# The end of a two-layer mixture-of-experts kernel: last rows completed from rows stored early, gathers issued together

## The chip, the cores and the metric

The kernel runs on one core of one Trainium2 chip. The metric is the device time of the whole program in microseconds (us); of several runs the median is given. Lower is better. All data is float32.

## The reference, cut to what matters

The program is a two-layer backbone: attention, then a grouped top-2 mixture of experts (MoE), with residual additions, and a final RMSNorm. The part around the change is the MoE of the second layer, with the residual addition and the final norm:

```python
def rms_norm(x, g):
    return x * rsqrt(mean(x * x, axis=-1) + 1e-6) * g

# h: 1024 tokens x 1024; every token has two experts with a gate each
y = ragged_dot(silu(ragged_dot(h[tok], w_gate)) * ragged_dot(h[tok], w_up), w_down)
y = y * gate                       # one row per (token, expert)
moe = zeros_like(h).at[tok].add(y) # two rows per token are summed
xl = xl + mod_l[5] * moe
out = rms_norm(xl, final_norm)
```

## The kernel before, in words

Tokens are sorted to experts by slots: each (token, expert) has a slot, and the tensor `slot_out` (`ys`) in HBM holds one finished row per slot, already gated and scaled by the modulation row. The experts stage of a layer (`experts`, L1679 on) works through items. An item is one expert with up to some hundred slots, or a block of 64 or 128 further slots. In the second layer (l = 1) F = 14 items are written out, then a loop `Fori(F, n)` handles blocks of 64 rows (once in this run), and a last item, one block of 128 slots at LASTB, is written out by itself.

TensorE (`last_item`, L1919) computes eight blocks b of gate and up products (L1929; 16 products of 128 x 128 each), then two halves of the down product (L1937), then a small product (L1942) that moves the rows of the last item to the place of the same tokens in a tile of their own. ACT takes silu of each block (L2050), VectorE multiplies it with the up part (`product`, L2163). Block b + 2 on TensorE waits for product b, since both use the same PSUM banks; the down products wait for the eighth product. Weights come in six pieces of 2 MB per item (`load_piece`, L1434 on: four of gate and up in two transfers each, two of down in one each), issued by SP into a ring of six buffers as soon as a piece's buffer is free.

While the last item is computed, the other tokens are finished. There are LT = 8 tiles t of 128 tokens. GpSimd gathers a tile's two rows per token from `slot_out` (`pairs`, L1808, indirect DMAs of 512 KB at L1813) into `pair[t]`: for the first tiles spare buffers, for tiles 3 to 7 ring buffers that must be free (`freed`, waits on `s_gu`). VectorE adds the two rows and then adds them to the residual x (`combined`, L2165, additions L2167 and L2169). ACT squares and sums (`square`, L2052). GpSimd takes the root (`root`, L1816, lines L1817 and L1819), VectorE scales (`scaled`, L2171, line L2176), and SP stores the tile (L1775). The slots of the last item are held at zero in `slot_out` (stored at L1754), so that all of this can run before the last item has a result.

The up to 128 tokens of the last item need their result added. Before: ACT stores each summed tile x to `x_rows` in HBM after its square (L2055, 8 stores of 512 KB). When all are stored, GpSimd gathers the 128 tokens' rows from `x_rows` into `zrow` (L1833). VectorE adds the small product (L2207, two halves), ACT squares (L2064), GpSimd takes the root, VectorE scales (L2211), and GpSimd scatters the rows to the output (L1839) when the eight tiles' stores have landed.

The order of work is written out by hand: each engine has one program, and semaphores tie them. GpSimd: pairs 0 to 2, then for each t: pairs t + 3, wait for the square of t, root t; then the gather from `x_rows`. ACT: silu 0 to 3, then for each t: square t, store t, silu t + 4. VectorE: products 0 to 2, combined 0, product 3, combined 1, then for b = 4 to 7: product b, combined b - 2, scaled b - 4; then the rest of combined and scaled with the two halves of gated rows (`gated_rows`, L2179, line L2183) between.

Of the kernel before, what the change touches and what calls it, by code (L numbers as in the profile page):

```python
# [8 lines left out]
I32 = mybir.dt.int32  # L9
# [4 lines left out]
P = 128  # L14
# [121 lines left out]
def build(nc, a):  # L136
# [3 lines left out]
    toep = dram("toep", [3, BLOCK_W, 16 * DROWS, BLOCK_W])  # L140
    h_dram = dram("h_rows", [NTOK, D])
    x_rows = dram("x_rows", [SEQ, D])
    ys = dram("slot_out", [-(-max(SLOTS) // P) * P, D])

    top = ExitStack()
# [21 lines left out]
    with top:  # L167
# [1511 lines left out]
        def experts(l, ring, p_in, token, gate, xg, s_xg):  # L1679
# [31 lines left out]
            with ExitStack() as c:  # L1711
# [12 lines left out]
                if l == 1:  # L1724
                    at_z = rows[:, 2, HALF:HALF + 4]
                    at_zi = slots[:, LT:NT, :].rearrange("p t i -> p (t i)")
                    flat = lambda q, r: ring[:, q, :, :].rearrange("p k f -> p (k f)")[:, r * D:(r + 1) * D]
                    pair = ((x[:, LT, :], x[:, LT + 1, :]), (yr[:, 1, :], yr[:, 2, :]), (xg[:, 1, :], xg[:, 2, :]),
                            (flat(0, 0), flat(0, 1)), (flat(0, 2), flat(0, 3)), (flat(1, 0), flat(1, 1)), (flat(1, 2), flat(1, 3)),
                            (flat(2, 0), flat(2, 1)))  # L1730
                    freed = (0, 0, 0, 2, 2, 4, 4, 6)
                    zrow, zjunk = flat(2, 2), flat(2, 3)
                    same = aT[:, 0, P:2 * P]
                    final_row = rows[:, 1, :]
                    s_pair = [sem(c, f"y_in{n}") for n in range(LT)]
                    (s_zero, s_zs, s_nr, s_xz, s_zx, s_zxT, s_zc, s_id, s_sum, s_x, s_ss, s_rs, s_h, s_xs, s_out, s_back, s_my, s_zz,
                     s_zss, s_zo, s_fin) = (sem(c, n) for n in (
                        "last_zero", "last_cleared", "final_row_in", "last_x_gathered", "last_x_transposed", "last_xT_ready", "last_token_steps",
                        "last_tokens_along", "pair_sum", "x_added", "ss_done", "rstd_steps", "out_rows", "x_stored", "out_stored",
                        "last_x_back", "last_shared", "last_x_steps", "last_ss", "last_out", "last_out_stored"))  # L1740
                block = c.enter_context(nc.Block())
                gub = lambda j, b, w: bank((b % 2) * 2 + w, 0, room(j))
                yb = lambda j, d: bank(4 + d % 2, 0, room(j))
# [4 lines left out]
                @block.sync  # L1748
                def _(sp):
                    n = count(sp)  # L1750
                    if l == 1:
                        sp.dma_start(final_row, a["final_norm"].partition_broadcast(P)).then_inc(s_nr, 16)
                        sp.wait_ge(s_zero, 1)
                        sp.dma_start(ys[SLOT0[l][F]:SLOT0[l][F] + P, :], yr[:, 2, :]).then_inc(s_zs, 16)  # L1754

                    with sp.Fori(1, n) as i:
                        e = sp.value_load(table[0:1, bass.ds(i, 1)], min_val=0, max_val=NE - 1)
                        for q in range(6):

                            if q < 4:  # L1760
                                sp.wait_ge(s_gu, i * 8 + 2 * q + 2)
                            else:
                                sp.wait_ge(s_y, i * 8 + 4 * (q - 4) + 4)
                            load_piece(sp, l, ring, p_in, e, q)
                    if l == 1:
                        e = sp.value_load(table[0:1, 63:64], min_val=0, max_val=NE - 1)
                        for q in range(6):
                            if q < 4:
                                sp.wait_ge(s_gu, n * 8 + 2 * q + 2)
                            else:  # L1770
                                sp.wait_ge(s_y, n * 8 + 4 * (q - 4) + 4)
                            load_piece(sp, l, ring, p_in, e, q)
                        for t in range(LT):
                            sp.wait_ge(s_h, t + 1)
                            sp.dma_start(grid_rows(out[0], t), pair[t][0]).then_inc(s_out, 16)  # L1775
                        sp.wait_ge(s_out, 16 * LT)
# [19 lines left out]
                def _(pool):  # L1796
                    n = count(pool)
                    pool.sem_inc(s_xt, 4)
                    for j in range(1, F + 1):
                        gather(pool, j)  # L1800
                        if l == 1 and j == F - 2:
                            nc.gpsimd.indirect_dma_start(out=xg[:, 1, :], out_offset=None, in_=h_dram,
                                                         in_offset=bass.IndirectOffsetOnAxis(token[:, LASTB:LASTB + 1], 0)).then_inc(s_xz, 16)
                    with pool.Fori(F, n) as j:
                        gather(pool, j + 1)
                    if l == 1:
# [15 lines left out]
                        pool.wait_ge(s_zx, 4)  # L1822
                        pool.wait_ge(s_st, OLD_ST + stored(n))
                        pool.sem_inc(s_go, 1)
                        for t in range(3):
                            pairs(t)
                        for t in range(LT):
                            if t + 3 < LT:
                                pairs(t + 3)
                            pool.wait_ge(s_ss, t + 1)  # L1830
                            root(t)
                        pool.wait_ge(s_xs, 16 * LT)
                        nc.gpsimd.indirect_dma_start(out=zrow, out_offset=None, in_=x_rows,  # L1833
                                                     in_offset=bass.IndirectOffsetOnAxis(token[:, LASTB:LASTB + 1], 0)).then_inc(s_back, 16)
                        pool.wait_ge(s_zss, 1)
                        root(LT)
                        pool.wait_ge(s_zo, 1)
# [175 lines left out]
                def _(act):  # L2013
# [32 lines left out]
                    if l == 1:  # L2046
# [5 lines left out]
                        def square(t):  # L2052
                            act.wait_ge(s_x, t + 1)
                            nc.scalar.activation(pair[t][1], x[:, t, :], ACT.Square, accum_out=ss[:, t:t + 1]).then_inc(s_ss, 1)
                            act.dma_start(x_rows[t * P:(t + 1) * P, :], x[:, t, :]).then_inc(s_xs, 16)  # L2055

                        for b in range(4):
                            silu(b)
                        for t in range(LT):
                            square(t)  # L2060
                            if t + 4 < FB:
                                silu(t + 4)
                        act.wait_ge(s_zz, 2)
                        nc.scalar.activation(zjunk, zrow, ACT.Square, accum_out=ss[:, LT:LT + 1]).then_inc(s_zss, 1)  # L2064
                    act.wait_ge(s_st, OLD_ST + stored(n))
# [3 lines left out]
                def _(dve):  # L2069
# [89 lines left out]
                    def last_item():  # L2159
# [23 lines left out]
                            nc.vector.scalar_tensor_tensor(out=yr[:, 0, cols], in0=bank(4 + h), scalar=gate[:, 0, LASTB:LASTB + 1],  # L2183
                                                           in1=rows[:, 0, cols], op0=ALU.mult, op1=ALU.mult).then_inc(s_yr, 1)

                        for b in range(3):
                            product(b)
                        combined(0)
                        product(3)
                        combined(1)  # L2190
                        for b in range(4, FB):
                            product(b)
                            combined(b - 2)
                            scaled(b - 4)
                        combined(6)
                        scaled(4)
                        combined(7)
                        gated_rows(0)
                        scaled(5)
                        scaled(6)  # L2200
                        gated_rows(1)
                        scaled(7)
                        dve.wait_ge(s_back, 16)
                        for h in range(2):
                            cols = slice(h * HALF, (h + 1) * HALF)
                            dve.wait_ge(s_my, h + 1)
# [116 lines left out]
```

## Time and profile before

| | |
|---|---|
| median of 3 runs | 4063.71 us (4054.61, 4063.71, 4065.64) |
| the profiled execution, its own time | 4054.0 us |
| its span | 4052.2 us |
| TensorE busy (matmul) | 3765.5 us, 93% |
| VectorE busy | 1239.8 us, 31% |
| ACT busy | 760.5 us, 19% |
| GpSimd busy | 404.1 us, 10% |
| read from and written to HBM | 547.56 MB and 77.47 MB |

The profile is one execution, recorded instruction by instruction; its span is from the first to the last instruction. Times in it are counted from the start of the span. Engines are PE (TensorE matmuls), PEld (TensorE weight loads), DVE (VectorE), ACT (ScalarE), POOL (GpSimd) and SP; a name with q, as SPq, is that engine's issue of a DMA. DMA queue q1 is SP's, q10 is ACT's, q0 is GpSimd's. An f32 matmul is recorded as two instructions, so a block of 16 products is 32 records. "issue" as the reason of a wait means that the profile shows nothing that the engine waited for. DMA figures are of packets that move over 16 transfer engines.

### The profile page before, as it was taken

To read this page: it belongs to the slowest core of one execution; us is meant where nothing else is said; L and a number is where in the kernel's file an instruction comes from. 1 tells how busy PE (TensorE), PEld (TensorE's weight loads), DVE (VectorE), ACT (ScalarE), POOL (GpSimd) and SP (SyncE) were. 2 spreads that over 40 slices of the span, in tenths; PEclk is the share of its full clock that TensorE was granted. 3 is DMA by queue.
4 is the path that set the end of the run, shared out by engine and by line. 5 is a ranking of instruction groups with operands and counts; after the bars stand their busy time and mean duration, and the time that the engine had idled before them with its cause. 6 is when DMAs were issued, how large, how long until landed. Compare 5 with 4: busy or idle time off the path is not lost. (4 is left out here: it accounts for less than half of the span.)

```text
span 4052.2 us, 53671 instructions
## 1 busy us (share of the span) xinstructions
PE 3765.5 (93%) x22338; PEld 2858.8 (71%) x22338; DVE 1239.8 (31%) x3166; ACT 760.5 (19%) x1668; POOL 404.1 (10%) x400
## 2 busy tenths in 40 slices
PE   6999999999699999999958999999989699999996
PEld 3656767645577899998835666666655678899774
DVE  3233333322411112211153555555532401101113
ACT  2222333311000000000022333333321000000001
POOL 3001000023000000000031111011014000000002
PEclk7999999998799999999969999999998799999998
DMA  5458500110744466779741000000101748867988
GB/s 161 164 210 327 188 21 26 53 35 39 250 141 146 164 204 231 263 264 306 261 145 33 12 16 17 17 16 16 48 12 42 258 160 271 289 206 254 316 296 323
DMA packets 450551, 628.09 MB, mean 155 GB/s; under 512 B 25928, under 2 KB 343752, under 8 KB 444048
## 3 DMA queue, kind: packets, MB, share of 16 engines
q1 hardware_dynamic: 420504, 514.83, 38.4%
q0 software_dynamic: 21008, 79.37, 5.3%
q10 hardware_dynamic: 8808, 30.49, 2.1%
q8 instruction: 183, 3.00, 0.3%
q14 instruction: 48, 0.39, 0.0%
HBM read 547.56 MB, written 77.47 MB: 154 GB/s over the span
## 5 line engine op out<-in xcount | busy, mean ns | idle before, releaser
L1960 PE MATMUL ps<-item_xT,expert_ring 128*128 128x128 f32 (+9 forms) x7168 | 1054.4, 310 | 1.1 <-DVE item_xT L2078 1.1
L1960 PEld LDWEIGHTS ps<-item_xT,expert_ring 128*128 128x128 f32 x7168 | 1000.3, 191 | 56.9 <-issue 5.5
L1997 PE MATMUL ps<-item_aT,expert_ring 128*128 128x144 f32 (+8 forms) x2304 | 405.1, 331 | 0.0
L1997 PEld LDWEIGHTS ps<-item_aT,expert_ring 128*128 128x128 f32 x2304 | 356.9, 192 | 24.1
L2223 DVE TENSOR_TENSOR item_aT<-item_silu,ps 128x128 f32<-128x128 f32 (+9 forms) x224 | 74.5, 333 | 962.1 <-ACT item_silu L2034 962.1
L2034 ACT ACTIVATE item_silu<-ps 128x128 f32<-128x128 f32 (+9 forms) x224 | 70.2, 313 | 1150.1 <-PE ps L1960 1150.1
L732 PE MATMUL ps<-hT,w_group 128*128 128x512 f32 (+1 forms) x704 | 254.7, 515 | 0.5 <-PEq L297 0.5
L377 PE MATMUL ps<-hT,oT 128*128 128x512 f32 x576 | 251.5, 596 | 1.4 <-PEq L982 0.7
L1076 PE MATMUL ps<-hT,w_group 128*128 128x512 f32 (+1 forms) x576 | 232.4, 546 | 0.5 <-PEq L297 0.5
L377 PEld LDWEIGHTS ps<-hT,oT 128*128 128x128 f32 x576 | 109.2, 191 | 134.7 <-issue 134.7
L1790 POOL DMA_INDIRECT gathered<-h_rows,slot_tokens x48 | 49.5, 1031 | 1542.9 <-PE ps L1868 1537.1
L1125 PE MATMUL ps<-df_kT,df_qT 64*128 64x512 f32 (+1 forms) x768 | 188.3, 567 | 14.9 <-DVE df_max L1354 8.5
L732 PEld LDWEIGHTS ps<-hT,w_group 128*128 128x128 f32 x704 | 130.4, 190 | 100.8 <-issue 95.0
L1076 PEld LDWEIGHTS ps<-hT,w_group 128*128 128x128 f32 x576 | 106.1, 190 | 99.8 <-issue 97.3
L1141 PEld LDWEIGHTS ps<-df_V,rows 128*128 128x128 f32 x1280 | 154.0, 195 | 17.9 <-issue 16.1
L1141 PE MATMUL ps<-df_V,rows 128*128 128x128 f32 x1280 | 157.5, 279 | 0.9 <-ACT rows L1268 0.9
L1085 PE MATMUL ps<-w_group,hT 128*128 128x128 f32 x1280 | 152.1, 277 | 0.0
L1085 PEld LDWEIGHTS ps<-w_group,hT 128*128 128x128 f32 x1280 | 146.3, 192 | 7.0 <-issue 7.0
L741 PE MATMUL ps<-w_group,hT 128*128 128x128 f32 x1280 | 146.5, 275 | 0.0
L741 PEld LDWEIGHTS ps<-w_group,hT 128*128 128x128 f32 x1280 | 144.7, 192 | 0.1
L1354 DVE CUSTOM_DVE_ANT_0 rows<-ps,df_zero 128x512 f32<-128x512 f32 x180 | 107.8, 599 | 120.3 <-PE ps L1125 120.3
L1987 PE MATMUL ps<-expert_ring,item_aT 128*128 128x512 f32 x320 | 139.1, 593 | 0.0
(315 smaller groups left out, 3951.4 us busy)
## 6 DMA issues: line engine op xcount, KB each, us to landing
expert_ring<-in_expert_w_gate SPq DMA_DIRECT2D x128, 1024.0 KB, 5.2
expert_ring<-in_expert_w_up SPq DMA_DIRECT2D x128, 1024.0 KB, 8.1
expert_ring<-in_expert_w_down SPq DMA_DIRECT2D x64, 2048.0 KB, 9.8
oT<-in_mod_w SPq DMA_DIRECT2D x40, 1024.0 KB, 6.4
slot_out<-rows POOLq DMA_DIRECT2D x9, 4096.0 KB, 39.2
w_group<-in_w_qkv SPq DMA_DIRECT2D x48, 512.0 KB, 3.8
slot_out<-item_y ACTq DMA_DIRECT2D x31, 512.0 KB, 7.5
h_rows<-hr SPq DMA_DIRECT2D x18, 512.0 KB, 2.6
```

Of the source, the lines that this page charges most:

```text
L377: m = nc.tensor.matmul(bank(n % 3), oT[:, k * NTOK + t * P:k * NTOK + (t + 1) * P], wo[:, k, h * HALF:(h + 1) * HALF], start=k == 0, stop= ...
L732: m = nc.tensor.matmul(bank(b, 0, w), wq[:, 0 if kind == "q" else 1, k, :], hT[:, k, c0:c0 + w], start=k == 0, stop=k == KD - 1)
L741: m = nc.tensor.matmul(bank(b, t * P, (t + 1) * P), hT[:, k, (c0 + t) * P:(c0 + t + 1) * P], wq[:, 2, k, :], start=k == 0, stop=k == KD - 1)
L1076: m = nc.tensor.matmul(bank(b, 0, w), wq[:, 0 if kind == "q" else 1, k, :], hT[:, k, c0:c0 + w], start=k == 0, stop=k == KD - 1)
L1085: m = nc.tensor.matmul(bank(b, t * P, (t + 1) * P), hT[:, k, (c0 + t) * P:(c0 + t + 1) * P], wq[:, 2, k, :], start=k == 0, stop=k == KD - 1)
L1125: nc.tensor.matmul(S(m, n), qT[r, par, t * P:(t + 1) * P], kT[r, par, c0:c0 + w], start=True, stop=True).then_inc(s_S, 1)
L1141: mm = nc.tensor.matmul(O, pT[:, i * P:(i + 1) * P], V[:, par, i, :], start=i == 0, stop=i == NT - 1)
L1354: nc.vector.tensor_tensor_reduce(out=maps(g, t)[m][:, c0:c0 + w], in0=S(m, n), in1=zero[:, 0:1].to_broadcast([P, w]), scale=1.0, scalar=NE ...
L1960: m = nc.tensor.matmul(gub(j, b, w), ring[:, b // 2, k, w * 256 + (b % 2) * P:w * 256 + (b % 2 + 1) * P], xT[:, k, 0:C], start=k == 0, sto ...
L1987: m = nc.tensor.matmul(bank(4 + h)[0:C], aT[:, f, 0:C], ring[:, 4 + h, f, :], start=f == 0, stop=f == FB - 1)
L1997: m = nc.tensor.matmul(yb(j, d), ring[:, 4 + d // 4, f, (d % 4) * P:(d % 4 + 1) * P], aT[:, f, 0:C], start=f == 0, stop=f == FB - 1)
L2223: nc.vector.tensor_tensor(aT[:, b, 0:C], sg[:, b % 2, 0:C], gub(j, b, 1), ALU.mult).then_inc(s_a, 1)
```

## The change

- A small tensor `slot_pairs` in HBM takes each token's two slots. SP stores it, and the eight tiles of x as they are before the experts' sum, into `x_rows`, at the start of the second layer's experts stage.
- GpSimd gathers the two slots of each of the last item's tokens into `at_zi[:, 0:2]`, ahead of its loop, and waits for them.
- GpSimd issues all eight pairs ahead of the first root. At t = 2 of its loop over roots, when all gate and up blocks are done, it gathers the last tokens' residual rows from `x_rows` and their two rows each from `slot_out`, into ring buffers 2 and 3.
- ACT no longer stores x. It takes silu 0 to 5, then for each t: silu t + 6, square t.
- VectorE takes products 0 to 5, combined 0, product 6, combined 1, product 7, and then the rest in the order of the diff. After the eighth scaling it adds the two gathered rows to `zrow`, one after the other, before the halves of L2207.

```diff
@@ build @@
+    slot_pairs = dram("slot_pairs", [SEQ, 2], I32)
@@ experts, l == 1 @@
+                    zpair = (flat(3, 0), flat(3, 1))
@@ sync @@
                         sp.wait_ge(s_zero, 1)
                         sp.dma_start(ys[SLOT0[l][F]:SLOT0[l][F] + P, :], yr[:, 2, :]).then_inc(s_zs, 16)
+                        sp.dma_start(slot_pairs.rearrange("(t p) i -> p t i", p=P), slots[:, 0:LT, :]).then_inc(s_xs, 16)
+                        for t in range(LT):
+                            sp.dma_start(x_rows[t * P:(t + 1) * P, :], x[:, t, :]).then_inc(s_xs, 16)
@@ gpsimd @@
+                    if l == 1:
+                        pool.wait_ge(s_xs, 16 * (LT + 1))
+                        pool.wait_ge(s_zc, 4)
+                        nc.gpsimd.indirect_dma_start(out=at_zi[:, 0:2], out_offset=None, in_=slot_pairs,
+                                                     in_offset=bass.IndirectOffsetOnAxis(token[:, LASTB:LASTB + 1], 0)).then_inc(s_pz, 16)
+                        pool.wait_ge(s_pz, 16)
                     with pool.Fori(F, n) as j:
                         gather(pool, j + 1)
...
-                        for t in range(3):
+                        for t in range(LT):
                             pairs(t)
                         for t in range(LT):
-                            if t + 3 < LT:
-                                pairs(t + 3)
+                            if t == 2:
+                                pool.wait_ge(s_gu, n * 8 + 16)
+                                pool.sem_inc(s_go, 1)
+                                nc.gpsimd.indirect_dma_start(out=zrow, out_offset=None, in_=x_rows,
+                                                             in_offset=bass.IndirectOffsetOnAxis(token[:, LASTB:LASTB + 1], 0)).then_inc(s_back, 16)
+                                for i in range(2):
+                                    nc.gpsimd.indirect_dma_start(out=zpair[i], out_offset=None, in_=ys,
+                                                                 in_offset=bass.IndirectOffsetOnAxis(at_zi[:, i:i + 1], 0)).then_inc(s_back, 16)
                             pool.wait_ge(s_ss, t + 1)
                             root(t)
-                        pool.wait_ge(s_xs, 16 * LT)
-                        nc.gpsimd.indirect_dma_start(out=zrow, out_offset=None, in_=x_rows,
-                                                     in_offset=bass.IndirectOffsetOnAxis(token[:, LASTB:LASTB + 1], 0)).then_inc(s_back, 16)
@@ scalar @@
-                            act.dma_start(x_rows[t * P:(t + 1) * P, :], x[:, t, :]).then_inc(s_xs, 16)
-
-                        for b in range(4):
+
+                        for b in range(6):
                             silu(b)
                         for t in range(LT):
+                            if t + 6 < FB:
+                                silu(t + 6)
                             square(t)
-                            if t + 4 < FB:
-                                silu(t + 4)
@@ vector @@
-                        for b in range(3):
+                        for b in range(6):
                             product(b)
                         combined(0)
-                        product(3)
+                        product(6)
                         combined(1)
-                        for b in range(4, FB):
-                            product(b)
-                            combined(b - 2)
-                            scaled(b - 4)
+                        product(7)
+                        for t in range(2, 5):
+                            combined(t)
+                            scaled(t - 2)
+                        gated_rows(0)
+                        combined(5)
+                        scaled(3)
                         combined(6)
-                        scaled(4)
+                        gated_rows(1)
                         combined(7)
-                        gated_rows(0)
-                        scaled(5)
-                        scaled(6)
-                        gated_rows(1)
-                        scaled(7)
-                        dve.wait_ge(s_back, 16)
+                        for t in range(4, LT):
+                            scaled(t)
+                        dve.wait_ge(s_back, 48)
+                        for i in range(2):
+                            if i:
+                                dve.wait_ge(s_zy, 1)
+                            nc.vector.tensor_tensor(zrow, zrow, zpair[i], ALU.add).then_inc(s_zy, 1)
+                        dve.wait_ge(s_zy, 2)
```

## Rows read from the trace of the kernel before

**Rows 1.** The page's head.

```profile
span 4052.2 us, 53671 instructions
```

**Rows 2.** The chain that ended last: start us, us, what.

```profile
4011.38 14.47 DMA expert_ring<-slot_out,slots
...
4031.99 7.77 DMA expert_ring<-x_rows,slot_tokens
...
4039.79 1.30 DVE expert_ring L2207 x2
...
4044.90 1.06 POOL out L1839
```

**Rows 3.** DMA queues: packets, MB; from 3987.5 to 3990, 4000 to 4002.5, 2060 to 2064.

```profile
q1 hardware_dynamic: 181, 0.34, 36.6%
q0 software_dynamic: 177, 0.66, 66.4%
...
q10 hardware_dynamic: 88, 0.29, 29.1%
...
q0 software_dynamic: 399, 1.46, 95.8%
```

**Rows 4.** Timeline of POOL: start us, us, what, [idle before and what ended it].

```profile
3931.52 0.18 POOL L1785 COPY item_tokens<-slot_tokens 128x1 int32 x1 [42.26 <-PE ps L1868]
...
3980.20 0.95 POOL L1813 DMA_INDIRECT x_res<-slot_out,slots  x1 [46.77 <-DMA slot_out<-item_y]
...
3996.61 1.54 POOL L1813 DMA_INDIRECT expert_ring<-slot_out,slots  x1 [0.18 <-issue]
...
4010.05 1.02 POOL L1813 DMA_INDIRECT expert_ring<-slot_out,slots  x1 [0.27 <-issue]
```

**Rows 5.** Timeline of DVE.

```profile
3990.92 1.23 DVE L2167 TENSOR_TENSOR x_res<-x_res 128x1024 f32<-128x1024 f32 x1 [7.87 <-DMA x_res<-slot_out,slots]
...
3993.32 0.28 DVE L2163 TENSOR_TENSOR item_aT<-item_silu,ps 128x128 f32<-128x128 f32 x1
...
4010.82 1.23 DVE L2167 TENSOR_TENSOR expert_ring<-expert_ring 128x1024 f32<-128x1024 f32 x1 [1.74 <-DMA expert_ring<-slot_out,slots]
4012.09 1.23 DVE L2169 TENSOR_TENSOR x_res<-x_res,expert_ring 128x1024 f32<-128x1024 f32 x1
4013.23 1.28 DVE L2176 SCALAR_TENSOR_TENSOR gathered<-x_res,rstd,rows 128x1024 f32<-128x1024 f32 x1
...
4028.28 0.74 DVE L2183 SCALAR_TENSOR_TENSOR item_y<-ps,rows 128x512 f32<-128x512 f32 x1
...
4028.94 2.47 DVE L2176 SCALAR_TENSOR_TENSOR expert_ring<-x_res,rstd,rows 128x1024 f32<-128x1024 f32 x2
```

**Rows 6.** Timeline of PE and of ACT.

```profile
3971.43 18.35 PE L1929 MATMUL ps<-item_xT,expert_ring 128*128 128x128 f32 x156
3990.91 0.50 PE L1929 MATMUL ps<-item_xT,expert_ring 128*128 128x128 f32 x3 [1.14 <-issue]
...
3993.65 13.93 PE L1929 MATMUL ps<-item_xT,expert_ring 128*128 128x128 f32 x96 [1.75 <-DVE item_aT L2163]
...
3982.45 0.28 ACT L2050 ACTIVATE item_silu<-ps 128x128 f32<-128x128 f32 x1 [3.30 <-PE ps L1929]
3990.96 0.28 ACT L2050 ACTIVATE item_silu<-ps 128x128 f32<-128x128 f32 x1 [8.23 <-DMA expert_ring<-in_expert_w_down]
```

**Rows 7.** Windows: us, engines busy (x instructions), granted PE clock, DMA share, GB/s.

```profile
3180.00:3200.00 20.00, 16.15 (x85) 14.03 (x86) 3.62 (x11) 1.86 (x3) 2.74 (x3) 0.66 0.37 120
...
3990.00:4000.00 10.00, 7.12 (x34) 6.95 (x35) 5.58 (x7) 2.74 (x6) 4.60 (x6) 0.66 1.03 406
```

**Rows 8.** DMA issues: KB each, us to landing; and a weight piece in SP's timeline.

```profile
toep<-in_rpb_pad SPq DMA_DIRECT2D x3, 124.0 KB, 10.3
...
3199.84 0.41 SPq L1438 DMA_DIRECT2D expert_ring<-in_expert_w_gate  x1
...
out<-expert_ring SPq DMA_DIRECT2D x5, 512.0 KB, 4.3
```

More of the change, by code:

```diff
@@ L1736, in experts @@
                     (s_zero, s_zs, s_nr, s_xz, s_zx, s_zxT, s_zc, s_id, s_sum, s_x, s_ss, s_rs, s_h, s_xs, s_out, s_back, s_my, s_zz,
-                     s_zss, s_zo, s_fin) = (sem(c, n) for n in (
+                     s_zss, s_zo, s_fin, s_pz, s_zy) = (sem(c, n) for n in (
                         "last_zero", "last_cleared", "final_row_in", "last_x_gathered", "last_x_transposed", "last_xT_ready", "last_token_steps",
                         "last_tokens_along", "pair_sum", "x_added", "ss_done", "rstd_steps", "out_rows", "x_stored", "out_stored",
-                        "last_x_back", "last_shared", "last_x_steps", "last_ss", "last_out", "last_out_stored"))
+                        "last_x_back", "last_shared", "last_x_steps", "last_ss", "last_out", "last_out_stored", "last_slots_in", "last_rows_summed"))
                 block = c.enter_context(nc.Block())
```

## The prediction

> **What bounds the kernel now.** I read the end of the run backwards, since nearly all of the edit lies there. The page gives a span of 4052.2 us [rows 1] against 4054.0 us for that execution and a median of 4063.7 us; the three runs shown differ by 11 us. Every sum below is made against the profiled execution and then carried to the median by subtraction.
>
> The chain of waits ends so: the last tiles' work goes through gathers of which the last, issued at 4011.38, takes 14.5 us to land, the gather of the last item's rows from x_rows takes 7.8 us alone, its completion by VectorE starts at 4039.79, and the final scatter is issued at 4044.90 [rows 2]. From 4039.79 to the end of the span are 12.4 us that the edit does not touch. So the question is when the two additions of line 2207 can start.
>
> Three things set that. First the transfers. While weights and gathers are both in flight the two queues send packets one for one, 177 against 181, so the gathers (4 KB packets) move 0.66 MB in 2.5 us and the weights 0.34; at 4000 the stores into x_rows take another 0.29 MB of 2.5 us [rows 3]. Second GpSimd's program order: eight gathers from 3980.20 on, then one pair only after each tile's root, the last pair at 4010.05 and 4011.38 [rows 2, 4], and the gather from x_rows only after the eighth root [rows 4]. Third VectorE: it sits idle before the first addition at 3990.92, and the fourth product (3993.32) stands behind that addition [rows 5]. TensorE pays for it: 1.75 us idle before its sixth block, then three blocks in 13.93 us [rows 6] where one block at full clock takes 0.28 + 3.30 = 3.58 us (spacing of two silus, [rows 6]), the granted clock being 0.66 over those 10 us [rows 7].
>
> **The change, part by part.**
>
> *Stores moved to the start of the layer's expert stage.* Eight 0.5 MB stores leave ACT's queue near the end and go on SP's, with one store of 1024 pieces of 8 bytes, ahead of SP's loop. SP's next piece load is at 3199.84; between 3180 and 3200 the transfer engines are 37% busy at 120 GB/s [rows 7, 8]. At the 0.40 MB per us that the tail reaches [rows 3], the 4.2 MB take 10.5 us. The small pieces: a copy into toep, 124 KB in 3968 pieces of 32 bytes, lands in 10.3 us [rows 8], so 1024 pieces are worth some 2.7 us, with 0 and 10.3 as ends. Begun near 3184 that is over by 3195 to 3205. The piece loaded at 3199.84 is used by TensorE's second item only, and the gate and up blocks of one item alone are 8 x 3.58 = 28.6 us, the down products behind them; the gathers for that item are in the same case. Cost nothing; if that cover went, at most 5 us.
>
> *Gather of the slot pairs.* On GpSimd, ahead of its loop, with a wait for it to land. Behind it stands only the gather of the loop's first item, before which GpSimd idles 42.26 us [rows 4]. The nearest landing is the 7.8 us of [rows 2]. Cost nothing.
>
> *Six products ahead of the first addition.* The trace shows an oddity that is covered today. TensorE's fourth block should end at 3971.43 + 4 x 3.58 = 3985.8, but ACT's fourth silu starts at 3990.96 after 8.23 us idle, and TensorE has a hole of 1.14 us labelled issue at 3990 and ends its fifth block at 3993.65 - 1.75 = 3991.9, where 3971.43 + 5 x 3.58 = 3989.3 was due [rows 6]. Neither waits for data that I can name; one instruction block being fetched through full queues would do it. Today this is hidden behind the fourth product. After the edit nothing waits for the additions, and the hole is exposed. I keep it in the sum: blocks six to eight from 3991.9 at 3.58 us end at 4002.7, the eighth product at 4003.3 (silu 0.28, product 0.28). Without the hole 4000.6; with the clock falling again for one block (3.4 us) 4006.8. I take 4003.3, since the code and the traffic up to 3990 are the same. A clock fall I think unlikely: it came after 1.75 us more of idleness that now goes. The first two additions (2.4 us each) fit between products six, seven and eight.
>
> The Trainium skill ("Runtime: NRT & Kernel Launch", Instruction fetch mechanics) says that instruction refill is hidden behind the sequencer's own issue pace. By that rule the hole would be something else and need not return, and the sum would start from 4000.6; the 1.14 us labelled issue speak against it.
>
> *All gathers at once.* Pairs five to eight need no root any more. GpSimd issues one gather in 0.95 us when VectorE is idle (3980.20) and leaves 0.3 between two (4010.05 + 1.02 to 4011.38). At 3996.61 it took 1.54 [rows 2, 4], 0.6 more, which I read as the rest of a running addition; the ends are 0.95 and 0.95 + 1.23 = 2.18, one whole addition. The sixteenth is out by about 4002, the first root by 4003.5, needed at 4005.7. The three gathers for the last rows (1.5 MB) then take until about 4012, and the third root, behind them, comes about 0.7 us too late for its scaling (0 to 3 us as ends). The addition at 4010.82 began in the middle of the gather of 4010.05 and took its usual 1.23 us [rows 4, 5], so I charge VectorE nothing. The Trainium skill ("SBUF — State Buffer", Who interferes with whom) has whichever of the two comes second block until the first is done, VectorE too. By that each of the some eight gathers beside additions could also hold VectorE for up to 0.94 us, and the end would come up to 7.5 us later; the trace agrees for GpSimd and not for VectorE.
>
> *Transfers.* 4.2 MB leave the tail and 1.6 MB is added, 0.5 of it in place of the old gather. A piece of down weights lands at 3990.96 [rows 6], which I take for the last but one; the last 2.1 MB at 0.34 / 2.5 = 0.137 MB per us are in by 4006, needed at 4003 + 7 = 4010. The first pair (1.05 MB) lands at 3990.9 [rows 5], and each further one 1.05 / 0.264 = 4.0 us later: the third 3999, fourth 4003, fifth 4007. With no weights left the gather queue alone moves 1.46 MB in 4 us [rows 3], shared with finished rows: sixth 4011, seventh 4014.5, eighth 4018, the last rows 4023. VectorE, by the next part, wants them at 4003.3, 4007, 4010.8, 4015.4, 4019, 4022.6 and 4029.8. Each is about 4 us ahead: the gathers stop being the bound.
>
> *VectorE after the eighth product, back to back.* One addition pair costs 1.27 + 1.14 = 2.41 us (starts 4010.82, 4012.09, 4013.23), a scaling 2.47 / 2 = 1.235, a half of gated rows 0.7 [rows 5]. Left are six pairs 14.5, eight scalings 9.9, two halves 1.4, and the two new additions on the last rows, each waiting for the one before, 2 x 1.27 = 2.5: together 28.3 us. 4003.3 + 28.3 + 0.7 for the root = 4032.3 against 4039.79: **7.5 us less**. The last store of finished rows starts 2.5 us before that and lands in 4.3 us [rows 8], ahead of the scatter 5.1 us after. ACT loses eight issues beside its squares: nothing.
>
> **Rivals.**
> 1. *The hole does not return*: 4000.6 + 28.3, plus about 1.5 because the roots now come nearer to their use: 4030.4, 9.4 us less, 4044.6 profiled. For it: no semaphore explains the hole. This is also the outcome by the skill's page above.
> 2. *GpSimd is late or the clock falls*: every gather meets an addition at 2.18 us, so first and third root come 3 us late, or blocks six and seven run at half clock. 1 to 4 us less, 4050 to 4053 profiled. For it: 0.66 at 3990 [rows 7], and 19 gathers ahead of the third root. If VectorE were held by the gathers as well, the skill's rule above, the end would come here or, at its worst, level with before.
> 3. *The edit gives the time back and more.* Mechanism: holes like that of ACT at 3990.96 (3990.96 - 3985.8 = 5.1 us) hit VectorE, ACT and GpSimd one after another while the queues stay full, where before they fell into idle time that has gone. It decides from two exposed (10.2 against 7.5: 2.7 us slower, 4057); three give 4062, four 4067. Against: only one such time is seen in the trace.
> 4. *No change in effect*: were the gathers needed as late as now. Against it: at 4000 stores hold 28% of the bytes, and they go. It has no chance of its own beside rival 2.
>
> **How the numbers follow.** Base 0.5 (4 to 8.5 us less), rival 1 0.22 (8.5 to 11), rival 2 0.2 (0 to 4), rival 3 0.08. The likeliest is 4054.0 - 7.5 = 4046.5 for a profiled run like this one and 4063.7 - 7.5 = 4056.2 for the median. The runs of before fall at 4054.6 and at 4064 to 4066, so a median may sit 10 us lower than that for the same kernel: low end 4054.6 - 9.4 = 4045, high end 4063.7 with no gain. About 0.3% (12.2 us) is what a measurement of this kernel can tell from no change. No case reaches 12.2 us of gain; with runs that differ by 11 us I allow 0.17 for it, mostly from rival 1. Slower by over 12.2 us needs four exposed holes: 0.04.
>
> **What would show it.** Right: no addition before the sixth product; TensorE without the wait of 1.75 us; VectorE with under 2 us idle from the eighth product to line 2207's additions; no waiting for pairs from the fourth on; 7 to 8 us off 4039.79. The hole at 3990 present: base; absent: rival 1. GpSimd gathers at 2 us each and VectorE waiting for rstd: rival 2. Holes labelled issue on VectorE or ACT: rival 3. VectorE waiting for the slot_out gathers after 4007 would make the transfer reckoning wrong, and a longer first item near 3190 the early stores.

## The result, and the profile after

| | before | after |
|---|---|---|
| median, us | 4061.56 (4051.75 to 4067.37, 22 runs) | 4053.05 (4044.56 to 4057.81, 22 runs) |
| the profiled execution, its own time | 4054.0 | 4045.93 |
| its span | 4052.2 | 4044.1 |
| last item's first product on TensorE | 3971.43 | 3972.87 |
| start of the additions of L2207 (L2225 after) | 4039.79 | 4031.52 |
| between these two | 68.36 | 58.65 |
| last item's first product to the final scatter | 73.47 | 63.74 |

The ratio of the times is 0.998, with a 95% interval of 0.9974 to 0.9986: 8.1 us less, between 5.7 and 10.6. It is not the quotient of the two medians, which differ by 8.5 us. Both are under the 0.3% (12.2 us) named in the prediction, and the interval is clear of no change. Three later executions, two of e5 and one of e6, took 4165 to 10837 us and are left out of the times and ratios given below.

The two profiles differ by 8.3 us at the additions and by 9.7 us from the last item's start on, because that item starts 1.44 us later after. Of this 1.34 us is there already at SP's load of `rt_bias` (3138.59 before, 3139.93 after), ahead of anything that the change touches. So everything below is counted from the last item's first product.

The chain of waits after (start us, us, what), for [rows 2]: between the last gather's issue and the additions no transfer is left in it.

```profile
4009.54 1.96 POOL expert_ring L1845
...
4013.93 0.74 DVE item_y L2196
...
4024.98 1.18 POOL std L1828
4026.24 1.48 POOL rstd L1830
4027.81 1.28 DVE expert_ring L2189
4029.09 1.14 DVE expert_ring L2220
4030.26 1.24 DVE expert_ring L2220
4031.52 1.30 DVE expert_ring L2225 x2
```

Where before had gathers of 14.47 and 7.77 us, VectorE's own queue stands, with two roots that it waits for.

TensorE's timeline, for [rows 6]: start us, us, what, [idle before, what ended it].

```profile
3972.87 28.85 PE L1943 MATMUL ps<-item_xT,expert_ring 128*128 128x128 f32 x256
4002.49 7.13 PE L1951 MATMUL ps<-expert_ring,item_aT 128*128 128x512 f32 x16 [0.77 <-DVE item_aT L2176]
4010.37 7.13 PE L1951 MATMUL ps<-expert_ring,item_aT 128*128 128x512 f32 x16 [0.76 <-DMA expert_ring<-in_expert_w_down]
```

ACT's timeline, the third to fifth silu.

```profile
3983.89 0.28 ACT L2064 ACTIVATE item_silu<-ps 128x128 f32<-128x128 f32 x1 [3.29 <-PE ps L1943]
3987.46 0.28 ACT L2064 ACTIVATE item_silu<-ps 128x128 f32<-128x128 f32 x1 [3.30 <-PE ps L1943]
3991.04 0.28 ACT L2064 ACTIVATE item_silu<-ps 128x128 f32<-128x128 f32 x1 [3.29 <-PE ps L1943]
```

All eight blocks are one stretch of 28.85 us, with silus 3.57 us apart: the wait of 1.75 us is gone, and so is the hole near 3990 that the prediction kept.

VectorE's timeline from the eighth product on, with the only two waits before the final additions.

```profile
4002.07 0.29 DVE L2176 TENSOR_TENSOR item_aT<-item_silu,ps 128x128 f32<-128x128 f32 x1 [0.83 <-ACT item_silu L2064]
4002.27 1.22 DVE L2180 TENSOR_TENSOR gathered<-gathered 128x1024 f32<-128x1024 f32 x1
...
4012.73 1.28 DVE L2189 SCALAR_TENSOR_TENSOR gathered<-x_res,rstd,rows 128x1024 f32<-128x1024 f32 x1 [0.79 <-POOL rstd L1830]
...
4027.81 1.28 DVE L2189 SCALAR_TENSOR_TENSOR expert_ring<-x_res,rstd,rows 128x1024 f32<-128x1024 f32 x1 [0.51 <-POOL rstd L1830]
4029.01 2.48 DVE L2220 TENSOR_TENSOR expert_ring<-expert_ring 128x1024 f32<-128x1024 f32 x2
```

Nothing waits for a pair, where before 1.74 us were spent on one [rows 5].

GpSimd's timeline, for [rows 4]: the first of the sixteen gathers, the one that took longest, the last, and the three for the last rows.

```profile
3981.71 0.94 POOL L1824 DMA_INDIRECT x_res<-slot_out,slots  x1 [46.87 <-DMA slot_out<-item_y]
...
3995.38 1.78 POOL L1824 DMA_INDIRECT expert_ring<-slot_out,slots  x1 [0.30 <-issue]
...
4001.20 0.93 POOL L1824 DMA_INDIRECT expert_ring<-slot_out,slots  x1 [0.30 <-issue]
...
4006.53 1.45 POOL L1842 DMA_INDIRECT expert_ring<-x_rows,slot_tokens  x1 [0.18 <-issue]
4008.29 0.95 POOL L1845 DMA_INDIRECT expert_ring<-slot_out,slots  x1 [0.30 <-issue]
4009.54 1.96 POOL L1845 DMA_INDIRECT expert_ring<-slot_out,slots  x1 [0.30 <-issue]
```

Windows, for [rows 7], with the same columns.

```profile
3180.00:3200.00 20.00, 14.68 (x73) 12.55 (x74) 5.24 (x11) 1.57 (x2) 3.94 (x4) 0.66 0.84 257
3990.00:4000.00 10.00, 10.00 (x92) 10.00 (x92) 4.42 (x6) 1.87 (x5) 7.56 (x9) 1.00 1.03 402
```

The early stores double the traffic of the first stretch (120 to 257 GB/s). In the second the clock stays at 1.00 instead of 0.66.

### The profile page after: what moved, and what is told of

Read it like the earlier page. It is cut to its first block and busy times, and to the rows that moved or that the text cites. A ratio compares the mean times of both kernels' runs of the same rounds, so it can differ in the third digit from the quotient of the medians.

```text
span 4044.1 us, 53680 instructions
## 1 busy us (share of the span) xinstructions
PE 3758.2 (93%) x22338; PEld 2854.5 (71%) x22338; DVE 1243.0 (31%) x3168; ACT 760.4 (19%) x1668; POOL 412.7 (10%) x403
```

## The experiments

Three parts are told apart. *Early*: x and the slot pairs stored at the stage's start, the last rows completed from them. *Gathers*: all sixteen issued ahead of the first root. *Products*: six ahead of the first addition. "Interval" is the last item's first product to the start of the final additions, the row of the table above that reads 68.36 and 58.65. Twelve versions ran in three groups, each beside its own runs of before (medians 4062.33, 4060.35 and 4062.63 of 35, 29 and 33 runs).

**e1, products alone.** Before, with ACT's and VectorE's order of after (ACT's part shown, shortened).

```diff
-for b in range(4): silu(b)
-for t in range(LT): square(t); silu(t + 4)
+for b in range(6): silu(b)
+for t in range(LT): silu(t + 6); square(t)
```

> The kernel before with one part of the change: six silus and products ahead of the first addition, and the new order of VectorE and ACT. Three theories. Chain: what counted was the gather of the last rows from x_rows behind the eighth root (7.8 us); it stays, and the gathers five to eight still wait for a root, which now comes later, so -1 to +2 us against the kernel before. Volume: the tail is bound by bytes, and none go, so 0. Products: TensorE's wait of 1.75 us and the half clock behind it (13.93 us for three blocks instead of 10.7) were what counted, so 4 to 5 us faster. In the profile all expect three blocks in 10.7 us.

**e2, gathers alone.**

```diff
-for t in range(3): pairs(t)
+for t in range(LT): pairs(t)
 for t in range(LT):
-    if t + 3 < LT: pairs(t + 3)
```

> The kernel before with all sixteen gathers ahead of the first root, nothing else. Chain: the first root now comes near 4003 behind sixteen gathers, and the sixth product stands behind the first scaling, so TensorE loses some us in its last blocks; pairs land earlier; -2 to +3 us in all. Volume: 0. Products: slower by what TensorE loses, 1 to 4 us.

**e3, early alone**: after, with all three orders of before (e1's and e2's edits reversed).

> The kernel after with the order of gathers, products and squares of before: only the early stores and the completion from early rows and two gathered output rows are left of the change. Chain: 5 to 8 us faster than before, most of the 8.1 us of the whole change. Volume: 3.1 MB less at 0.41 MB per us, 7.7 us faster, pairs landing 4 us apart instead of 5.2. Products: 3 to 4 us faster.

**e4, early and gathers**: after, with e1's edit reversed.

> The kernel after with the order of products, squares and scalings of before: early rows and all gathers at once. Chain: 4 to 7 us faster than before, less than e3 by what TensorE loses where the sixth product waits for the first root behind sixteen gathers. Volume: 7.7 us faster. Products: 3 us faster or less.

**e5, early and products**: after, with e2's edit reversed.

> The kernel after with the gathers of the eight tiles issued between the roots as before (two of the three parts: early rows and products). Late-gather theory: in e1 VectorE waited 0.8 to 3.5 us for each of the pairs five to eight, issued after a root that itself comes later; that stays here, only with less traffic, so from the last item's first block to line 2207's additions some 62 to 65 us where after has 58.7 and before 68.4, and 3 to 6 us less than before in time. Rival, parts add up by themselves: e1 gave +2.7 and e3 -4.7, so 66.4 us, 2 us less than before.

**e6, gathers and products**: before, with e1's and e2's edits.

> The kernel before with gathers at once and six products ahead, but with the late stores and the gather from x_rows behind the eighth root. Serial-gather theory: additions are ahead and VectorE is busy through, but 8 to 9 us of gather stand behind the last root and the 4.2 MB of stores slow the last pairs: 65 to 68 us in the same interval, 0 to 3 us less than before. Rival, parts add up: e1 +2.7 and e2 -1.0 give 70.1 us.

**e7 and e12**: before and after unchanged.

> The kernel before, unchanged, for a second profile. Fetch theory of the prediction (the hole of 5 us on ACT and of 2.6 us on TensorE near 3990 belongs to this program's instruction stream): it is there again at the fourth silu. Rival: it belongs to that one execution and is gone, as in the profiles of the kernel after and of e1 to e4.

> The kernel after, unchanged, beside e9 to e11 on the same chip. 7 to 9 us less than before, 58.5 to 59 us from the last item's first block to line 2225, and no hole in ACT's silus.

| | time, us | ratio (95%) | interval, us |
|---|---|---|---|
| e7, before | 4063.49 (one run) | | 67.35 |
| e1, products | 4063.55 | 1.0006 (0.9998 to 1.0015) | 71.06 |
| e2, gathers | 4062.23 | 1.0006 (0.9998 to 1.0015) | 67.37 |
| e3, early | 4059.55 | 0.9994 (0.9986 to 1.0003) | 63.66 |
| e4, early, gathers | 4060.14 | 0.9996 (0.9987 to 1.0005) | 66.39 |
| e5, early, products | 4059.43 | 0.9996 (0.9986 to 1.0006) | 66.61 |
| e6, gathers, products | 4062.13 | 1.0005 (0.9995 to 1.0014) | 67.76 |
| e12, after (all three) | 4051.86 | 0.9976 (0.9968 to 0.9985) | 58.65 |

The intervals are of one profile each; before was profiled twice (68.36 and 67.35) and after twice (58.65 both times). Counted against e7, the parts alone give +3.7, 0.0 and -3.7 us, and the sum of them is 0; together they give -8.7. Any two give at most 1.0 us, less than early alone. In the times only the full set is clear of no change. Each incomplete version shows the wait that takes the place of the one removed. Nor do the parts add in twos: added up, they give 67.4 for e5, 71.1 for e6 and 63.7 for e4, where 66.6, 67.8 and 66.4 were measured. So e5's nearness to the 66.4 that its rival expected is no sign for that rival. Of the theories named for e1 to e4, the one by chain expected 5 to 8 us from e3 and the one by volume 7.7; its interval gave 3.7. The one by products expected 3 to 4 there, but also 4 to 5 from e1, which lost 3.7.

Products alone: TensorE runs its eight blocks through, but the first square now comes after seven silus instead of four, so the first root is late, and each later pair stands behind a root. GpSimd's timeline of e1:

```profile
4007.65 0.38 POOL L1817 TENSOR_SCALAR std<-ss 128x1 f32<-128x1 f32 x1 [8.27 <-ACT x_res L2054]
...
4009.86 1.03 POOL L1813 DMA_INDIRECT expert_ring<-slot_out,slots  x1 [0.18 <-issue]
...
4024.18 0.94 POOL L1813 DMA_INDIRECT expert_ring<-slot_out,slots  x1 [0.30 <-issue]
```

and VectorE's of e1, which waits 0.83, 3.46, 2.72 and 1.83 us for pairs and then for the gather from `x_rows`:

```profile
4026.38 1.23 DVE L2167 TENSOR_TENSOR expert_ring<-expert_ring 128x1024 f32<-128x1024 f32 x1 [3.46 <-DMA expert_ring<-slot_out,slots]
...
4051.99 1.29 DVE L2207 TENSOR_TENSOR expert_ring<-expert_ring,ps 128x512 f32<-128x512 f32 x2 [6.33 <-DMA expert_ring<-x_rows,slot_tokens]
```

Gathers alone (e2): TensorE waits 4.01, 2.13 and 3.84 us for products, and VectorE 1.84, 1.99 and 1.20 us for pairs, then 6.73 us for the gather from `x_rows`.

Early with the old orders: TensorE waits for products that stand behind additions, so its eighth block is late. The three gathers of the last rows wait 5.21 us for that block on GpSimd, the third root and pairs seven and eight stand behind them, and VectorE waits for these. Timelines of TensorE and VectorE of e3:

```profile
4003.25 9.04 PE L1945 MATMUL ps<-item_xT,expert_ring 128*128 128x128 f32 x64 [3.87 <-DVE item_aT L2178]
...
4023.91 15.78 PE L1953 MATMUL ps<-expert_ring,item_aT 128*128 128x512 f32 x32 [7.45 <-DVE item_aT L2178]
...
4022.23 1.34 DVE L2191 SCALAR_TENSOR_TENSOR gathered<-x_res,rstd,rows 128x1024 f32<-128x1024 f32 x1 [3.06 <-POOL rstd L1830]
...
4030.94 1.23 DVE L2182 TENSOR_TENSOR expert_ring<-expert_ring 128x1024 f32<-128x1024 f32 x1 [2.92 <-DMA expert_ring<-slot_out,slots]
```

With e2's order added (e4) TensorE waits 3.95, 2.28 and 6.96 us in the same places, and the three gathers 6.03 us for the eighth block. The root behind them holds VectorE for 4.59 us, and the late second down product for another 3.73 us. Early and products without the gathers (e5): pairs seven and eight are issued behind the three gathers of the last rows. VectorE's timeline of e5:

```profile
4020.38 1.34 DVE L2191 SCALAR_TENSOR_TENSOR gathered<-x_res,rstd,rows 128x1024 f32<-128x1024 f32 x1 [3.06 <-POOL rstd L1830]
...
4030.85 1.23 DVE L2182 TENSOR_TENSOR expert_ring<-expert_ring 128x1024 f32<-128x1024 f32 x1 [4.21 <-DMA expert_ring<-slot_out,slots]
```

Gathers and products without early (e6): VectorE waits 1.63, 2.18 and 1.85 us for pairs, then 6.45 us for the gather from `x_rows`.

The hole near 3990: e7, the kernel before once more, has ACT's silus evenly spaced where [rows 6] had 8.23 us idle. ACT's timeline of e7:

```profile
3989.39 0.28 ACT L2050 ACTIVATE item_silu<-ps 128x128 f32<-128x128 f32 x1 [3.30 <-PE ps L1929]
3992.97 0.28 ACT L2050 ACTIVATE item_silu<-ps 128x128 f32<-128x128 f32 x1 [3.30 <-PE ps L1929]
3996.54 0.28 ACT L2050 ACTIVATE item_silu<-ps 128x128 f32<-128x128 f32 x1 [3.30 <-PE ps L1929]
```

Of 14 profiles one has the hole. It belongs to that execution and not to the code, and it cost that execution next to nothing: TensorE resumes after its wait 22.2 us into the item there and 22.0 us in e7, since both wait for the product behind the first addition. The 68.36 - 67.35 = 1.0 us between the two intervals arises at the fourth to eighth pairs, which landed later; from the fifth on their gathers were also issued later.

**e8, stores back in the tail.** After, and ACT also stores each x to a tensor that nobody reads.

```diff
+act.dma_start(x_again[t * P:(t + 1) * P, :], x[:, t, :]).then_inc(s_again, 16)
```

> The kernel after with ACT's eight stores of 512 KB put back behind the squares, into a tensor of their own that nobody reads. Lead theory (pairs land about 4 us ahead of VectorE, so the first part of any added traffic is free): 4.2 MB at 0.41 MB per us are 10 us of transfer, of which 3 to 6 us reach the end. Volume theory (the tail is bound by bytes): 9 to 10 us slower than after. VectorE theory taken strictly: 0 to 1 us slower than after.

4058.24 us, ratio 1.0000 (0.9991 to 1.0009), interval 64.79: 6.1 us of the 8.7 are gone by putting 4.2 MB of stores back. Beside e6 (67.76), where the last rows' gather also stands behind the eighth root, it tells two halves of *early* apart: 3.0 us for taking that gather out of the chain (less what the two gathers added for it cost) and 6.1 us for the traffic. The stores are 10.5 us of transfer at 0.40 MB per us, so some 4 us were in hand, as the prediction reckoned for the pairs. VectorE's timeline of e8, the first and the last of four waits (2.11, 1.39, 1.31, 1.84):

```profile
4016.08 1.22 DVE L2183 TENSOR_TENSOR expert_ring<-expert_ring 128x1024 f32<-128x1024 f32 x1 [2.11 <-DMA expert_ring<-slot_out,slots]
...
4031.79 1.22 DVE L2183 TENSOR_TENSOR expert_ring<-expert_ring 128x1024 f32<-128x1024 f32 x1 [1.84 <-DMA expert_ring<-slot_out,slots]
```

**e9, VectorE's two additions left out**: the last rows then lack what the other expert gives, and only the time is of use.

```diff
-for i in range(2):
-    nc.vector.tensor_tensor(zrow, zrow, zpair[i], ALU.add).then_inc(s_zy, 1)
```

> The kernel after without VectorE's two additions of the gathered output rows to the last item's residual rows (those rows' other expert is left out of the output). VectorE theory: the queue is without idle time from the eighth product on, so the two additions count in full, 2.5 us less than after, 56.2 us from the last item's first block to line 2225 instead of 58.7. Transfer theory: the last rows land when VectorE wants them, and the time stays within 0.5 us of after.

4051.30 us, ratio 0.9975 (0.9965 to 0.9985), beside 0.9976 for e12: the times cannot tell the two apart. The profile can: the interval is 56.14, 2.5 us less, all of VectorE's 2.48, so VectorE's queue is what sets the interval. From the item's start to the scatter it is 61.63 against 63.75, 2.1 us less. The scatter begins 0.7 us after the last scaling, where the kernel after has 0.3. GpSimd's timeline of e9:

```profile
4041.98 1.06 POOL L1853 DMA_INDIRECT out<-expert_ring,slots  x1 [2.12 <-DVE expert_ring L2224]
```

The scatter also waits for the stores of the eight tiles; the DMA view of e9 shows their packets running until about 4041, so the last store probably takes over here. That was not isolated.

**e10, the last rows summed by TensorE**: products with the identity matrix add the residual row and both expert rows in PSUM ahead of the small product; ACT and VectorE read PSUM.

```diff
+pe.wait_ge(s_back, 48)
+for h in range(2):
+    for i, src in enumerate((zrow, *zpair)):
+        nc.tensor.matmul(bank(6 + h), ident, src[:, cols(h)], start=i == 0, stop=False)
```

> The kernel after with the completion of the last item's rows on TensorE: residual rows and the two gathered rows are summed in PSUM by products with the identity, with the small product on top, and ACT's square and VectorE's scaling read PSUM. VectorE loses 2.5 + 1.3 us. VectorE theory: the scatter then waits for the last store of finished rows, issued with the eighth scaling and landing 4.4 us later, so 3 us less than after. Rival, the completion only moves: TensorE's seven products of 128 x 512 and ACT's square come behind the second half of gated rows and the scatter comes at the same time, 0 to 1 us less.

4053.51 us, ratio 0.9979 (0.9970 to 0.9987): no better than e12. From the item's start to the scatter 64.59 against 63.75. TensorE's timeline of e10:

```profile
4017.57 7.13 PE L1952 MATMUL ps<-expert_ring,item_aT 128*128 128x512 f32 x16 [1.22 <-DMA expert_ring<-in_expert_w_down]
4031.28 7.44 PE L1958 MATMUL ps<-expert_ring,con 128*128 128x512 f32 x12 [6.58 <-DMA expert_ring<-slot_out,slots]
```

The rows land 51.7 us after the item's start, at 4024.5 in the frame of after, where VectorE wants them at 4029.0. So the sum moved onto an engine that was free does not help: it has to wait for the rows, and it then runs at the lower clock. The windows of e10 (columns as in [rows 7]):

```profile
4022.00:4031.00 9.00, 2.70 (x7) 0.92 (x5) 8.90 (x9) 2.82 (x5) 5.71 (x5) 0.87 0.83 339
4031.00:4035.00 4.00, 3.71 (x5) 1.68 (x6) 3.49 (x4) 0.63 (x2) 2.64 (x2) 0.50 0.53 142
4035.00:4039.00 4.00, 4.00 (x11) 1.70 (x10) 0.83 (x1) 0.00 (x0) 0.00 (x0) 0.95 0.98 345
```

**e11, two tiles' sums there as well**: e10, with tiles 6 and 7 summed by TensorE instead of VectorE.

```diff
+for t in (6, 7):
+    for h in range(2):
+        for i, src in enumerate((x[:, t, :], *pair[t])):
+            m = nc.tensor.matmul(bank((t - 6) * 2 + h), ident, src[:, cols(h)], start=i == 0, stop=i == 2)
```

> As e10, and the sums of tiles 6 and 7 (x and both output rows) on TensorE too, six products of 128 x 512 for each, in the banks that gate and up have left. VectorE loses 4.8 us more. VectorE theory: 4 to 5.5 us less than after. Rival: transfers bound by then (pair eight lands some 4 us ahead of its use in after), so no more than 4 us less than after.

4053.92 us, ratio 0.9981 (0.9973 to 0.9990); item to scatter 65.46. Kept busy, TensorE does the last rows' 12 records in 5.31 us instead of 7.44, but a tile costs it 5.15 us against 2.4 on VectorE: each f32 product of 512 columns is two records, 0.86 us together. TensorE's timeline of e11, one tile's first half and the last rows:

```profile
4022.28 1.02 PE L1960 MATMUL ps<-x_res,con 128*128 128x512 f32 x2
4023.14 1.88 PE L1960 MATMUL ps<-expert_ring,con 128*128 128x512 f32 x4
...
4032.58 5.31 PE L1966 MATMUL ps<-expert_ring,con 128*128 128x512 f32 x12
```

VectorE then waits 3.35, 3.87 and 5.65 us for roots. The 3 us that e10 and the 4 to 5.5 us that e11 were to give did not come; of the versions with a whole output none beats the kernel after.

## Why the prediction held, and where it did not

**The mechanism held.** The transfers stopped being the bound and VectorE's queue became it: no addition before the sixth product, no wait for any pair, and 1.30 us idle between the eighth product and the additions (under 2 was asked). Its work there was priced at 28.3 us. Measured from the end of the eighth product (4002.36) to 4031.52 it is 29.16, with 1.30 of waiting in it, so 27.9 of work.

**The step that failed is the hole.** The prediction said "the hole is exposed. I keep it in the sum", 2.7 us, "since the code and the traffic up to 3990 are the same". e7 has the same code and traffic and no hole, nor has any other of the 14 profiles but one. The eighth product ended 29.5 us into the item, against 31.9 in the sum (4003.3 less 3971.43). The base's interval comes to 60.9 us (4032.3 less 3971.43); measured are 58.65: 2.4 less for the hole, 0.4 less of VectorE's work, 0.6 more of waiting for roots. So rival 1 came true (0.22 was given to it): its 59.0 us (4030.4 less 3971.43) stands against 58.65, measured twice. The gain in the interval is 9.7 us against the profile that the prediction was made from (rival 1 said 9.4) and 8.7 us against e7; the ratios of the times give 8.1 and, in the third group, 9.8. A single oddity without a releaser should have been set against the even spacing of every other row, not carried over whole.

The Trainium skill ("Runtime: NRT & Kernel Launch", Instruction fetch mechanics) has refill mostly hidden. The runs agree so far as the hole does not return. The prediction's guess was an instruction block fetched through full queues. The DMA view shows such a block in every one of the 14 profiles, 14.5 to 15.5 us into the item, just where ACT's fourth silu was due. DMA queues (packets, MB, share) of before, 3985 to 3987.5, with the hole, and of after, 3987.5 to 3990, without it:

```profile
q8 instruction: 1, 0.02, 2.6%
...
q8 instruction: 1, 0.02, 2.6%
```

So such a block alone does not make the hole, and in before it moved no later than elsewhere (14.5 to 15 us into the item). What caused it that once stays open.

**Roots.** 0.7 us of waiting was in the sum, at the third root. There it was 0.79, as priced, after the three gathers; the other 0.51 is at the eighth scaling. The root's multiplication takes 1.43 to 1.53 us beside VectorE's work and 0.55 without it, and at the eighth tile nothing lies between it and its use. Rival 1's 1.5 us covered this.

**GpSimd and VectorE.** The sixteenth gather was out at 4002.13, as said (by about 4002), or 1.3 us earlier than said, counted from the item's start. Of all nineteen three took 1.45 to 1.96 us, inside the range of 0.95 to 2.18; others beside additions (3998.72 to 4001.20) kept their 0.93 to 0.95, so the charge was rather too high. VectorE's addition at 3998.70 ran over two gathers and took 1.27 us, the others 1.21 to 1.23. The Trainium skill ("SBUF — State Buffer", Who interferes with whom) has whichever comes second wait; as predicted, the trace of after agrees in part for GpSimd and not for VectorE, and rival 2 did not come.

**Transfers.** Right in kind, and wrong in two sizes that cost nothing here. The last piece of the down weights was to be in by 4006, 34.6 us into the item, and needed 38.6 us into it; it landed at 4010.37, 37.5 us into it, and without the hole was wanted 0.76 us earlier. TensorE waits for that long, covered by the 3.01 us that it idles later, before its last product. With all gathers issued the two queues stay at one packet for one. DMA queues of after, 4000 to 4002.5 (packets, MB, share):

```profile
q0 software_dynamic: 179, 0.61, 62.5%
q1 hardware_dynamic: 179, 0.37, 38.5%
```

The last rows were to land at 4023, 51.6 us into the item, and by e10 they do after 51.7. They are wanted at 4029.0, so 4.5 us are in hand where 6.8 were claimed with the hole in the sum. e8 gives about 4 for the whole queue.

**Early stores.** Priced at nothing, 5 us at most. SP's timeline of after:

```profile
3184.62 0.35 SPq L1754 DMA_DIRECT2D rows<-in_final_norm  x1
...
3186.49 7.43 SPq L1759 DMA_DIRECT2D x_rows<-x_res  x8
3201.27 0.40 SPq L1439 DMA_DIRECT2D expert_ring<-in_expert_w_gate  x1
```

From the load of `final_norm` to the next piece are 16.65 us (16.72 before: 3199.84 [rows 8] less 3183.12, where that load starts), and to the last item's start 788.25 (788.31 before): nothing, as said.

**Rivals 3 and 4.** No hole on any engine in either profile of after. The change without effect did not come, but e1, e2 and e6 show how near it was: without the early stores, new orders give nothing or cost 3.7 us.

**The numbers.** 4053.05 us lies 3.2 below 4056.2 and inside the range. The gain, 8.1 us by the ratio with 7.5 forecast, and 9.8 in the third group, stays under 12.2: within 0.3%, as the 0.79 said. That 8.1 lies in the base's span of 4 to 8.5 us and not in rival 1's is luck, since the hole by which the two differ was absent: 7.5 was a sum that ended 2.2 us too late. The distance of the times has another part, the base: before's median over 22 runs is 4061.56, not the 4063.71 of three.

**What stays open.** The experts stage from `final_norm` to the last item takes 788.3 to 788.4 us in the first profile of before, in both of after and in e5 and e8 to e11, and 791.9 to 793.1 in e1 to e4, e6 and e7. Of the 3.6 us between e7 and before, 3.2 lie in two runs of 32 TensorE records that went slower: 8.78 us for 7.09 just before the last item, where the granted clock was 0.81 instead of 1.00, and 6.55 for 5.04 near 3660. All seven profiles of kernels with both early and products are among the short ones, and of the seven others one is, so this may be more than chance. But e8 is among the short ones too and its time equals that of before (ratio 1.0000, at most 3.7 us less), and the ratios of after (8.1 and 9.8 us) leave little over beside the interval's 8.7 to 9.7. So I do not count it as an effect of the change; one profile of each version can't settle it.

## What to carry to other kernels

When a tail is bound by several queues that take turns, try an order for all of them at once: three parts that alone cost 3.7 us, gave nothing and gave 3.7 us (71.1, 67.4 and 63.7 us against 67.4) were worth 8.7 us together, and any two of them at most 1.0, since each passed the wait to the next queue. Data that is known early and added late, as the residual here, can leave the busiest stretch for a quiet one, and be completed with what was already being gathered. Before a stall seen in one profile enters a sum, look whether anything released it; if not, give it a chance, not a place.

## What was not expected of the hardware

- A stall of ACT (4.9 us beyond the even spacing of its silus) and of TensorE (2.4 us: five blocks in 20.5 us, 18.1 in e7) with no releaser appeared in one profile of 14 and in no other.
- A wait of 6.58 us on TensorE was followed by a granted clock of 0.50 (1.2 GHz): 12 records took 7.44 us instead of 5.31. So in e10 the sum by TensorE was dearest just where the engine had been idle.
- On GpSimd a 128 x 1 multiplication took 0.55 us alone and up to 1.61 (before, at 3999.75) beside VectorE's 128 x 1024 additions and scalings, nearly three times as much, while the additions took 1.21 to 1.23 us and at most 1.30 (e1).
